# A two-layer decoder trunk in split fp32: thirteen projection units stream act_hi and act_lo as one 512-column operand, nine of them in two half-width passes over their first four ticks

## What is computed

```python
def reference(x, ...):
    for layer in range(2):
        h = rmsnorm(x, norm_pre_mix[layer])
        if layer % 2 == 0:
            y = gmlp_dilated_layer(h, ab_w_in[0], ...)   # h @ (2048 x 5120), gMLP gate, 8 heads, @ (2048 x 2048)
        else:
            y = stick_breaking_layer(h, sb_w_in[0], sb_w_out[0])  # h @ (2048 x 6144), 16 heads, @ (2048 x 2048)
        x = x + rmsnorm(y, norm_post_mix[layer])
        h = rmsnorm(x, norm_pre_ffn[layer])
        y = squared_relu_mlp(h, ffn_w1[layer], ffn_w2[layer])
        x = x + rmsnorm(y, norm_post_ffn[layer])
    return x
```

## Time and profile before

| | before |
|---|---|
| runs, us | 2183.65, 2183.61, 2182.11 |
| median, us | 2183.61 |
| profiled execution, its own time, us | 2182.25 |
| profiled execution, span, us | 2180.4 |
| instructions | 30479 |
| PE matmul, busy | 2163.5 us, 99% |
| PE weight load, busy | 1891.5 us, 87% |
| DVE, busy | 1236.5 us, 57% |
| ACT, busy | 1016.1 us, 47% |
| HBM read | 403.47 MB, 186 GB/s over the span |

### The profile page before, as it was taken

The page is one execution under the profiler, slowest core; times in us unless marked ns, Lnnn a source line. Parts: engine busy times, 40 slices in busy tenths (PEclk is TensorE's granted clock), DMA queues, the critical chain, the costliest instruction groups (busy, mean ns, idle before and its releaser), DMA issues.

```text
span 2180.4 us, 30479 instructions
## 1 busy us (share of the span) xinstructions
PE 2163.5 (99%) x12017; PEld 1891.5 (87%) x12017; DVE 1236.5 (57%) x1187; ACT 1016.1 (47%) x1097; POOL 18.7 (1%) x22
## 2 busy tenths in 40 slices
PE   9999999999999999999999999999999999999998
PEld 7999888888888888888899999888888888888886
DVE  5556567555554555555655555566545645554555
ACT  5444345543443443454535545564434534443543
POOL 0000000000000000000000000000000000000000
PEclk9999999999999999999999999999999999999999
DMA  9555555566556556655454555555566565656553
GB/s 310 188 174 174 194 174 156 182 203 193 189 187 191 183 193 212 192 192 193 155 194 155 173 173 188 170 156 184 191 194 192 175 211 174 199 192 210 187 193 116
DMA packets 202768, 406.73 MB, mean 187 GB/s; under 512 B 6400, under 2 KB 7744, under 8 KB 202176
## 3 DMA queue, kind: packets, MB, share of 16 engines
q1 hardware_dynamic: 202272, 405.37, 57.3%
q10 hardware_dynamic: 416, 0.23, 0.0%
HBM read 403.47 MB, written 2.10 MB: 186 GB/s over the span
## 4 chain that ended last, share of the span: by engine, by line
PE 96%; DVE 2%; issue 0%; ACT 0%; DMA 0%; POOL 0%; POOLq 0%; DVEq 0%; SPq 0%; ACTq 0%
PE ps L1061 96%; DVE w_lo L652 1%; DVE act_pair L700 0%; PE ps L1145 0%; DVE tmp L730 0%; DVE x_sb L692 0%; DMA w_raw<-in_ab_w_in_dram 0%; POOL rst L327 0%; ACT act_pair L389 0%; PE ps L1217 0%; ACT tmp L428 0%; ACT w_hi L357 0%; DVE tmp L954 0%; PE ps L1196 0%; DVE bn L995 0%
## 5 line engine op out<-in xcount | busy, mean ns | idle before, releaser
L652 DVE TENSOR_TENSOR w_lo<-w_raw,w_hi 128x1024 fp32r<-128x1024 f32 x752 | 914.2, 1225 | 832.9 <-ACT w_hi L357 822.5
L357 ACT ACTIVATE w_hi<-w_raw 128x1024 fp32r<-128x1024 f32 x752 | 789.6, 1059 | 997.4 <-PE ps L1061 992.0
L1061 PE MATMUL ps<-act_pair,w_hi 128*128 128x256 f32 (+1 forms) x3968 | 854.4, 337 | 0.5 <-issue 0.4
L1061 PEld LDWEIGHTS ps<-act_pair,w_hi 128*128 128x128 f32 x3968 | 664.6, 190 | 64.4 <-issue 1.7
L1061 PE MATMUL ps<-act_pair,w_lo 128*128 128x256 f32 x2944 | 557.4, 283 | 0.0
L1061 PE MATMUL ps<-w_hi,hid_hi 128*128 128x512 f32 x1280 | 499.9, 391 | 0.0
L1061 PE MATMUL ps<-w_hi,hid_lo 128*128 128x512 f32 x1280 | 498.1, 389 | 0.0
L1061 PE MATMUL ps<-w_lo,hid_hi 128*128 128x512 f32 x1280 | 498.0, 389 | 0.0
L1061 PEld LDWEIGHTS ps<-act_pair,w_lo 128*128 128x128 f32 x2944 | 457.6, 191 | 18.7
L1061 PEld LDWEIGHTS ps<-w_hi,hid_lo 128*128 128x128 f32 x1280 | 240.2, 188 | 50.3
L1061 PEld LDWEIGHTS ps<-w_hi,hid_hi 128*128 128x128 f32 x1280 | 240.3, 188 | 49.3
(11 more groups left out here) (108 smaller groups left out, 573.7 us busy)
## 6 DMA issues: line engine op xcount, KB each, us to landing
w_raw<-in_ffn_w_dram SPq DMA_DIRECT2D x256, 1024.0 KB, 5.3
w_raw<-in_sb_w_in_dram SPq DMA_DIRECT2D x48, 1024.0 KB, 5.1
w_raw<-in_ab_w_in_dram SPq DMA_DIRECT2D x39, 1024.0 KB, 5.1
w_raw<-in_ab_w_out_dram SPq DMA_DIRECT2D x16, 1024.0 KB, 5.1
w_raw<-in_sb_w_out_dram SPq DMA_DIRECT2D x16, 1024.0 KB, 5.1
gpost<-in_norm_post_mix_dram SPq DMA_DIRECT2D x2, 1024.0 KB, 7.3
gpost<-in_norm_post_ffn_dram SPq DMA_DIRECT2D x2, 1024.0 KB, 6.8
out_dram<-x_sb SPq DMA_DIRECT2D x3, 512.0 KB, 2.7
```

The costliest lines, as they stand in the source:

```text
L357: nc.scalar.activation(w_hi[:, t % RING, :, :], w_raw[:, t // 2, h:h + 2, :], ACT.Copy).then_inc(hi_ready, 1)
L652: nc.vector.tensor_tensor(w_lo[:, t % RING, :, :], w_raw[:, t // 2, h:h + 2, :], w_hi[:, t % RING, :, :].bitcast(F32), ALU.subtract).then_ ...
L1061: return nc.tensor.matmul(dst, lhsT, rhs, start=start, stop=stop, skip_group_check=True)
```

## The change

Units 2 to 5, 7, 8, the k unit of layer 1's first group, and q and k of its three looped groups, thirteen in all, go from tick_features to the pair form. Units 2, 3, 7 and 47 run tick_pairs for all their ticks; the other nine (4, 5, 8 and the six of the loop) run `pair_unit`. It has to make do with banks 0 to 5, of which it takes four while two are still to be evacuated. So it runs ticks 0 to 3 for two feature blocks, then ticks 0 to 3 again for the other two, and from tick 4 on plain tick_pairs. The ring's slots 0 to 3 are therefore given back only in the second pass. Its waits for hi_ready and lo_ready are for two ticks at once.

ACT's copy of the half-sum (`rest`) and DVE's add (`add_rest`) stand ahead of c(u+1, 3), and DVE's scaling of the sum behind it. Extras of steps 9 and 10 move to step 8, which now runs between the post and c(u+1, 4). The scales' transposes go from tick 4 to tick 5, and DVE's copy of them into the first unit's step 6. Outputs use other banks in turn (OUT_BUF).

```diff
-OUT_BUF = [0, 1, 2, 0]
+OUT_BUF = [1, 2, 0, 1]
...
 # ACT
+                    if ended and t == TICKS - 1:
+                        ended()
                     conv_at(u, t)
                 post()
...
-                        10: [lambda: l1_weights(0, grp), lambda: l1_soft_hi(1, grp)],
+                        8: [lambda: l1_weights(0, grp), lambda: l1_soft_hi(1, grp)],
...
+            def rest(u, dst, first):
+
+                unit_finished(u)
+                nc.scalar.activation(dst[:, :, :], bank4_halves(first)[1], ACT.Copy).then_inc(a_rest, 1)
...
 # DVE
-                if k:
-                    scale_tiles(k)
...
-                          9: [lambda: l1_exponent(0, grp), lambda: l1_softplus(1, grp)],
+                          8: [lambda: l1_exponent(0, grp), lambda: l1_softplus(1, grp)],
...
+            def add_rest(dst, first, n):
+
+                dve.wait_ge(a_rest, n)
+                nc.vector.tensor_tensor(dst[:, :, :], bank4_halves(first)[0], dst[:, :, :], ALU.add).then_inc(a_sum, 1)
+                dve.wait_ge(a_sum, n)
+
+            def scaled_q(src):
+                nc.vector.scalar_tensor_tensor(qT[:, :, :], src, SCALE, rs_tiles, ALU.mult, ALU.mult
+                                               ).then_inc(post_done, 1)
...
+            def qkv_group(u, extras, q_bank, k_bank, v_buf, n):
+                posts = ((lambda: add_rest(qT, q_bank, n), lambda: scaled_q(qT[:, :, :])),
+                         (lambda: add_rest(kT, k_bank, n + 1), scaled_k),
+                         (lambda: post_v(u + 2, v_buf), None))
...
 # PE
-                keep_busy(0 if k == 2 else 2, 6)
+                keep_busy(0, 6)
...
-                if k and s == 4:
+                if k and s == 5:
                     transpose_scales(k)
...
+            def pair_unit(u, first, halves, extras, second_free):
+
+
+                pe.wait_ge(post_done, u - 1)
+                for n, half in enumerate(halves):
+                    for s in (0, 2):
+                        for f in extras.get(2 * n + s // 2, []):
+                            f()
+                        if n and s == 0:
+                            second_free()
+                        pe.wait_ge(hi_ready, 8 * u + s + 2)
+                        for kt in range(2 * s, 2 * s + 4):
+                            for f in half:
+                                mm(ps[:, first + f, :], w_hi[:, kt // 2, kt % 2, f * P:(f + 1) * P],
+                                   act_pair[:, kt, :, :], kt == 0, False)
+                        pe.wait_ge(lo_ready, 8 * u + s + 2)
+                        for kt in range(2 * s, 2 * s + 4):
+                            for f in half:
+                                last = mm(ps[:, first + f, 0:T], w_lo[:, kt // 2, kt % 2, f * P:(f + 1) * P],
+                                          act_hi[:, kt, :], False, False)
+                            if n and kt % 2:
+                                last.then_inc(pe_ticks, 1)
+                for s in range(RING, TICKS):
+                    for f in extras.get(s, []):
+                        f()
+                    tick_pairs(first, s, s % RING, act_hi, act_lo, 8 * u + s + 1)
...
-            unit(2, tick_features, 0)
-            unit(3, tick_features, 1)
-            qkv_group(4, {1 + m: [lambda m=m: mix(m)] for m in range(4)})
-            qkv_group(7, l0_extras(0))
+            pe.wait_ge(s_scales, 1)
+            pe.wait_ge(s_prep, 3)
+            unit(2, tick_pairs, 4)
+            unit(3, tick_pairs, 0)
+            pair_unit(4, 2, (high, low), {1 + m: [lambda m=m: mix(m)] for m in range(4)}, lambda: summed(2))
+            pair_unit(5, 0, (low, high), {}, lambda: summed(3))
+            unit(6, tick_tokens, 2)
+            extras = l0_extras(0)
+            unit(7, tick_pairs, 0, extras=part_extras(extras, 0))
+            pair_unit(8, 2, (high, low), part_extras(extras, 1), lambda: summed(5))
+            unit(9, tick_tokens, 0, extras=part_extras(extras, 2))
...
-            qkv_group(U_IN1, {}, fresh=2)
+            unit(U_IN1, tick_features, 0, fresh=2)
+            pe.wait_ge(s_scales, 3)
+            unit(U_IN1 + 1, tick_pairs, 2)
+            unit(U_IN1 + 2, tick_tokens, 0)
             with pe.Fori(1, L1_GROUPS) as g:
-                qkv_group(U_IN1 + 3 * g, l1_extras(g - 1))
+                u, extras = U_IN1 + 3 * g, l1_extras(g - 1)
+                pair_unit(u, 0, (high, low), part_extras(extras, 0), lambda: pe.wait_ge(post_done, u))
+                pair_unit(u + 1, 2, (high, low), part_extras(extras, 1), lambda: summed(2 * g + 6))
+                unit(u + 2, tick_tokens, 0, extras=part_extras(extras, 2))
```

More of the change, by code:

```diff
@@ L365, in conv_at, with unit @@
                     conv(u + 1, t - 4)
-            def unit(u, post, extras=None, first=1):
+            def unit(u, post, extras=None, first=1, ended=None):
                 for t in range(first, TICKS):
@@ L519, in ready @@
                         act.wait_ge(pe_ticks, 8 * u0 + 32)
-                transition(k, u0 + 4, [ps[:, b, :] for b in range(TB)], ready)
+                transition(k, u0 + 4, [ps[:, 2 * OUT_BUF[3] + b, :] for b in range(TB)], ready)
             def ffn(u0, layer):
@@ L620, in _ @@
             for j in range(2):
-                unit(2 + j, lambda j=j: gelu_u(j))
-            qkv_group(4, {m + 2: [lambda m=m: gate_hi(m)] for m in range(4)})
-            qkv_group(7, l0_extras(0))
+                unit(2 + j, lambda: gelu_u(j), ended=lambda: rest(2 + j, (qT, kT)[j], 4 - 4 * j))
+            qkv_group(4, {m + 2: [lambda m=m: gate_hi(m)] for m in range(4)}, 2, 0)
+            qkv_group(7, l0_extras(0), 0, 2)
             out_phase(U_OUT0, l0_extras(1), 1)
@@ L629, in suffix_matrices @@
                 nc.scalar.activation(sum_mats[:, :], cst[:, P:3 * P], ACT.Copy).then_inc(s_sums, 1)
-            qkv_group(U_IN1, {9: [suffix_matrices]})
+            unit(U_IN1, nothing)
+            unit(U_IN1 + 1, nothing, {1: [suffix_matrices]}, ended=lambda: rest(U_IN1 + 1, kT, 2))
+            unit(U_IN1 + 2, nothing)
             with act.Fori(1, L1_GROUPS) as g:
-                qkv_group(U_IN1 + 3 * g, l1_extras(g - 1))
+                qkv_group(U_IN1 + 3 * g, l1_extras(g - 1), 0, 2)
             out_phase(U_OUT1, l1_extras(L1_GROUPS - 1), 3)
@@ new lines, in scaled_q, with scaled_k, post_v @@
+            def scaled_q(src):
+                nc.vector.scalar_tensor_tensor(qT[:, :, :], src, SCALE, rs_tiles, ALU.mult, ALU.mult
+                                               ).then_inc(post_done, 1)
+            def scaled_k():
+                nc.vector.tensor_tensor(kT[:, :, :], kT[:, :, :], rs_tiles, ALU.mult).then_inc(post_done, 1)
+            def post_v(u, buf):
+                unit_finished(u)
+                for b in range(TB):
+                    last = nc.vector.tensor_scalar(v_sb[:, b, :], ps[:, 2 * buf + b, :], rst[:, 6 + b:7 + b], None,
+                                                   ALU.mult)
+                last.then_inc(post_done, 1)
@@ new lines, in qkv_group, with whole_post @@
+            def qkv_group(u, extras, q_bank, k_bank, v_buf, n):
+                posts = ((lambda: add_rest(qT, q_bank, n), lambda: scaled_q(qT[:, :, :])),
+                         (lambda: add_rest(kT, k_bank, n + 1), scaled_k),
+                         (lambda: post_v(u + 2, v_buf), None))
+                for i, (ended, post) in enumerate(posts):
+                    def whole_post(i=i, post=post):
+                        if post:
+                            post()
+                        for f in extras.get(8 * i + 8, []):
+                            f()
+                    unit(u + i, whole_post, {t - 8 * i: f for t, f in extras.items() if 8 * i < t < 8 * i + 8},
+                         ended=ended)
@@ L918, in post @@
                                                 ALU.subtract).then_inc(post_done, 1)
-                    unit(u, post)
+                    unit(u, post, extras)
                 def group_up(g):
@@ L936, in add_y @@
                     return nc.vector.tensor_tensor(ys, ys, bank2(2 * par), ALU.add)
-                for j in range(4):
-                    up(0, j // 2, j % 2, fresh=j == 0)
+                up(0, 0, 0, fresh=True, extras={6: [lambda: scale_tiles(2 * layer + 1)]})
+                for j in range(1, 4):
+                    up(0, j // 2, j % 2)
                 dve.wait_ge(s_y0, layer + 1)
@@ L1039, in _ @@
             unit(1, lambda: stats_v(1), {1: [lambda: scale_rows(power_x)], 3: [lambda: scale_tiles(0)]})
-            unit(2, lambda: post_u(0), {1 + i: [lambda i=i: layernorm_v(i)] for i in range(3)})
-            unit(3, lambda: post_u(1))
+            unit(2, lambda: post_u(0), {1 + i: [lambda i=i: layernorm_v(i)] for i in range(3)},
+                 ended=lambda: add_rest(qT, 4, 1))
+            unit(3, lambda: post_u(1), ended=lambda: add_rest(kT, 0, 2))
             gates = {1: [lambda: gate(0)], 5: [lambda: gate_lo(3)]}
```

(7 more changed lines are left out.)

76 lines of the change are left out of this document (35 added, 41 removed).

## The result

| | before | after |
|---|---|---|
| median, us | 2182.19 (2181.84 to 2185.03, 20 runs) | 2186.86 (2186.65 to 2191.37, 20 runs) |
| ratio of the times | | 1.0024, 95% interval 1.0018 to 1.0030 |
| profiled execution, its own time, us | 2182.25 | 2188.25 |
| span, us | 2180.4 | 2186.5 |
| mean granted clock of the profiled execution | 0.999 | 0.997 |

The change made the kernel slower by 4.7 us by the medians, 0.21%, and by 0.24% by the ratio over all runs. The forecast was 2184.5 us and "no change that can be told"; the time lies 2.4 us above it, inside the range of 2177 to 2190, and just beyond the 0.2%, 4.4 us, that was set as the bound.

A forecast was written before the change was run, and what follows sets the result against it. PE, busy 99% of the span, was taken to bound the kernel. From 2182.25 us, -9.1 - 2.3 + 9.9 + 2.7 = +1.2 gave 2183.5 us, a median of 2184.5 expected; 8 in 10 range 2177 to 2190.

The forecast's parts named there:

- ticks of 13 units: PE's ticks in the thirteen converted units: 0.70 us less per unit, 9.1 us less PE work.
- transposes: Scales' transposes, first and third transition: PE's 1.5 us stand for DVE goes, 1.1 us gained in each, 2.3 us together.
- waits of the loop: Layer 1's three looped groups: PE waits 0.3, 2.4 and 0.6 us per group, 9.9 us in all.
- gate(0): Layer 0, unit 4: gate(0)'s first operation runs only after c(4, 4), so PE waits 2.7 us, once.
- It waits 2.4 us: Loop's k unit: PE wants w_hi of c(k, 3) at 29.0 us, there at 31.3 us; 2.4 us per group.
- The last step, to the median: From the summed 2183.5 us to the median: runs' median taken as 1.4 us above the profiled execution, 2184.5 us expected.
- Rival 1: Waits stay hidden in the loop, 1 us per group instead of 3.3: 2177 us, 2172 without waits; chance 0.26.
- Rival 2: Loop's k unit: the late chain grows, w_lo of c(k, 3), c(k, 4) and o_lo slip; 2188 to 2191 us; chance 0.19.
- o_lo's wait: Loop's k unit: o_lo ends at 44.4 us, l1_suffix(1) needs it at 43.8; PE waits 0.6 us per group.
- late chain: Loop: copy and add ending later than placed delay conversions and o_lo, every microsecond paid three times; decides from 4.4 us per group.
- Rival 3: Two-bank passes run at the features' pace: 2187.7 us, or 2193.6 if nothing is saved on starts; chance 0.03.
- the skill's rule: Warm matmuls stand their columns plus 2.5 ns apart: fewer starts save 2 us instead of 9.1; 2191.5 us.

The follow-up runs named there:

- E6: Changed kernel with gate(0) ahead of c(4, 4) on DVE and the loop's q and k units back in features form; median 2175.23 us, ratio 0.9967.
- E11: Changed kernel with gate(0) early, loop unrolled, q in features form, k in plain pair ticks over four free banks; median 2173.41 us, ratio 0.9960.
- E10: Kernel before with only the scales' transposes moved to tick 5 and DVE's copy of them to step 6; median 2179.91 us, ratio 0.9987.
- E3: Changed kernel with gate(0) put ahead of c(4, 4) on DVE; median 2185.66 us, ratio 1.0011.
- E1: Changed kernel with seven matmuls of a zeroed weight tile ahead of the wait for c(k, 3) in each looped k unit; median 2185.34 us, ratio 1.0012.
- E5: Changed kernel with gate(0) ahead of c(4, 4) and seven zero matmuls ahead of the loop's wait for c(k, 3); median 2181.3 us, ratio 0.9996.
- E7: Changed kernel with gate(0) early, the loop's q as a pair unit and its k in features form; median 2183.74 us, ratio 1.0007.
- E2: Changed kernel with ACT's copy and DVE's add put behind c(k, 3) in the loop's q units; median 2183.61 us, ratio 1.0001.
- E9: Kernel before with PE waiting ahead of k's tick 1 in each looped group until DVE's c(k, 3) is out; median 2186.4 us, ratio 1.0016.

## Why the prediction came out 2.4 us low

**The sum held.** Term by term:

| term | predicted, us | shown |
|---|---|---|
| ticks of 13 units | -9.1 | -8.3 to -8.7, 0.64 to 0.67 per unit: E6 and E11 have 7 and 10 such units at 7.0 and 8.9 us with the transposes, against 7.2 and 9.3, and E11's looped group is 0.64 us shorter |
| transposes | -2.3 | -2.3 by E10 |
| waits of the loop | +9.9 | 10.2 by the length of the group without a fall (3 x 3.4 with 0.70 per unit; 9.9 with 0.64); 7.2 on PE's rows, 9.3 on PEld's |
| gate(0) | +2.7 | 2.6 to 2.8; 2.5 by E3 |
| together, against 2182.25 | 2183.5 | 2183.7 without falls of the clock |

**The step that failed** is the one from a wait to its price: "It waits 2.4 us", "PE waits 2.7 us", each carried into the sum at its length. A wait of about 2 us here has a second price, matmuls at half clock behind it: 3.4 us of them, 1.5 us lost. Four such waits were forecast, and no term stood for what they do to the clock; "three groups wait 9.9 us" should have read 9.9 us and up to three falls, and the gate's wait one more. Typical runs have two by their step, 3.0 us. Against this the walk's overestimate of the wait itself (2.4 for 2.0 to 2.2) is small.

**The last step, to the median,** took 1.0 us too much and hid part of that: the three runs of before had their median at 2183.61, twenty have it at 2182.19, next to the profiled execution. So 2183.5 plus two falls is 2186.5, and 2186.86 was measured. By its own terms the prediction should have said 2183.5 + 1.4 = 2184.9, not 2184.5. That two errors of opposite sign, 3.0 us left out and 1.0 put in, leave the forecast 2.4 us off is in part luck.

**The rivals.** Rival 1 (waits stay hidden) is out: the logs start at 15.0 us into q and c(k, 3) is late by as much as was walked. Rival 2 foretold the right side and nearly the right time (2188), with the wrong mechanism: w_lo of c(k, 3) and c(k, 4) were in time, o_lo's wait was 0.4 to 0.6 us as placed, and E1 and E5 take back the excess without touching ACT or DVE. Where the late chain costs more than was placed is E7, at o_lo, a kernel that was not in question. Rival 3 is out: two-bank passes run at the pair form's pace. Of the skill's rule (the Trainium skill, TensorE: Matmul & The Clock Gate, section Back-to-back issue gap), which that section gives for isolated matmuls, and by which thirteen units would save 2 us, the runs show that it doesn't hold for these matmuls and loads: with it E6 would be at 2182.2 - 2.3 - 7 x 0.16 = 2178.8 us, and 2175.2 was measured.

**What stays open.** Of waits of 1.9 to 2.6 us six of the thirteen in the profiles were followed by a fall and the others, of the same length in the same place of the next group, were not; by their steps after's runs have from two to five falls. Waits of 1.1 to 1.2 us (E2, E9) and E7's three of up to 1.7 us were followed by none in the profiles taken, though most of E7's runs stand a step or two above its profiled one. What decides between them was not found. The fall in the first 20 us stands in the profiles of after, E7 and E9. These are also the three profiles of the thirteen in which PE waits for the DMA of the constants (shape_constants_dram) there, by 0.4 to 0.8 us, ahead of two waits of 0.7 to 1.6 us that all of them have. Whether that is its cause was not tested. Steps of 1.5 us show in the runs of before too (2182.1, 2183.6, 2185.0).
